# The first expert block is taken out of the block loop of a 32-expert layer and worked ahead of the block table

## What is computed

```
logits = (h @ w_router) + b_router            # [512, 32]
topv, idx = lax.top_k(logits, 4)
gates = softmax(topv)
# tokens grouped by expert; for every block of tokens of one expert e:
gu = xblk @ w_gate_up[e] + b_gate_up[e]       # 1024 -> 2048
gate, up = min(gu[:, :1024], 7), clip(gu[:, 1024:], -7, 7)
act = (up + 1) * gate * sigmoid(1.702 * gate)
y = act @ w_down[e] + b_down[e]               # 1024 -> 1024
out[token] += y * gate_weight
```

## Time and profile before

| | |
|---|---|
| median of 3 runs | 2981.27 us (2976.05 to 2981.37) |
| the profiled execution's own time | 2982.14 us |
| its span in the profile | 2980.3 us |
| TensorE busy | 2805.3 us, 94% |
| VectorE, ScalarE, GpSimd busy | 1319.7, 829.6, 103.1 us |
| read from and written to HBM | 572.91 MB, 29.88 MB |

### The profile page before, as it was taken

The page is one execution under the profiler, slowest core; times in us unless marked ns, Lnnn a source line. Parts: engine busy times, 40 slices in busy tenths (PEclk is TensorE's granted clock), DMA queues, the critical chain, the costliest instruction groups (busy, mean ns, idle before and its releaser), DMA issues.

```text
span 2980.3 us, 44597 instructions
## 1 busy us (share of the span) xinstructions
PE 2805.3 (94%) x16220; PEld 1781.0 (60%) x16221; DVE 1319.7 (44%) x2773; ACT 829.6 (28%) x1663; POOL 103.1 (3%) x118
## 2 busy tenths in 40 slices
PE   9999999988999989998999899999999999999999
PEld 7888668743333333333333387585787695666884
DVE  6774686442232222222222455535564454444662
ACT  3321662212222222222222223414121224323211
POOL 0000000000000000000000000011000000110000
PEclk9999999978999999999999999999999999999999
DMA  3224312257999999999999831031321321112212
GB/s 143 85 71 138 120 52 85 76 209 317 416 423 415 414 410 410 414 413 407 412 413 413 337 117 69 29 110 36 106 85 57 105 101 43 68 64 78 85 57 85
DMA packets 115239, 587.90 MB, mean 197 GB/s; under 512 B 12714, under 2 KB 18218, under 8 KB 89507
## 3 DMA queue, kind: packets, MB, share of 16 engines
q1 hardware_dynamic: 105890, 569.26, 48.4%
q0 software_dynamic: 9216, 16.90, 1.5%
HBM read 572.91 MB, written 29.88 MB: 202 GB/s over the span
## 4 chain that ended last, share of the span: by engine, by line
PE 80%; DMA 12%; DVE 5%; issue 2%; ACT 2%; DVEq 1%; ACTq 0%; SPq 0%; POOLq 0%
PE banks L422 37%; DMA arena<-in_w_experts 11%; PE banks L1757 11%; PE banks L355 5%; PE banks L1799 5%; PE banks L989 4%; PE banks L916 3%; PE banks L1765 2%; PE banks L1805 2%; PE banks L1004 2%; PE banks L978 2%; PE banks L294 1%; PE banks L1243 1%; PE banks L952 1%; PE banks L1736 1%
## 5 line engine op out<-in xcount | busy, mean ns | idle before, releaser
L422 PE MATMUL banks<-arena 128*128 128x256 f32 (+2 forms) x5376 | 1156.1, 376 | 12.7 <-ACT arena L459 6.0
L422 PEld LDWEIGHTS banks<-arena 128*128 128x128 f32 x5376 | 1005.4, 190 | 147.8 <-issue 14.1
L1757 PE MATMUL banks<-arena 128*64 128x512 f32 x2048 | 466.7, 601 | 48.4 <-DMA arena<-in_w_experts 34.2
L1757 PEld LDWEIGHTS banks<-arena 128*64 128x64 f32 x2048 | 156.2, 137 | 315.2 <-issue 313.0
L459 ACT ACTIVATE arena<-banks 128x512 f32<-128x512 f32 (+2 forms) x220 | 129.9, 590 | 699.5 <-PE banks L422 696.6
L407 DVE TENSOR_TENSOR arena<-arena 128x1024 f32<-128x1024 f32 (+2 forms) x220 | 235.8, 1072 | 50.6 <-issue 26.4
L1938 DVE TENSOR_TENSOR arena<-banks,arena 128x512 f32<-128x512 f32 x64 | 44.3, 692 | 462.7 <-PE banks L1783 236.5
L1799 PE MATMUL banks<-arena 128*64 128x512 f32 x1024 | 237.8, 600 | 1.6 <-DMA arena<-in_w_experts 1.1
L475 DVE TENSOR_TENSOR arena<-banks,arena 128x512 f32<-128x512 f32 (+2 forms) x123 | 83.5, 680 | 273.6 <-PE banks L422 269.8
L355 PE MATMUL banks<-arena 128*128 128x512 f32 x384 | 166.8, 592 | 0.0
L1799 PEld LDWEIGHTS banks<-arena 128*64 128x64 f32 x1024 | 67.6, 135 | 129.1 <-issue 129.1
(11 more groups left out here) (269 smaller groups left out, 2388.3 us busy)
## 6 DMA issues: line engine op xcount, KB each, us to landing
arena<-in_w_experts SPq DMA_DIRECT2D x192, 2048.0 KB, 24.1
arena<-in_w_in SPq DMA_DIRECT2D x76, 1024.0 KB, 4.9
arena<-in_w_out SPq DMA_DIRECT2D x12, 1024.0 KB, 5.0
arena<-in_w_branch SPq DMA_DIRECT2D x24, 512.0 KB, 4.6
expert_rows<-arena SPq DMA_DIRECT2D x1, 8192.0 KB, 30.2
arena<-expert_rows SPq DMA_DIRECT2D x4, 2048.0 KB, 18.0
arena<-in_w_in SPq DMA_DIRECT2D x2, 2048.0 KB, 9.1
arena<-in_w_in SPq DMA_DIRECT2D x4, 832.0 KB, 4.9
```

The lines of the kernel that those rows point to most:

```text
L422: last = PE.matmul(PS[:, bank, t * width:(t + 1) * width], one[:, t * P:(t + 1) * P], other, start=(first and t == 0 and kk == 0), stop=(t ...
L1757: last = PE.matmul(PS[HB * s:HB * (s + 1), 4 + h], xT[:, k, 0:HB], gate_up(2 * h + s, k), start=(k == 0), stop=(k == 7))
```

## The change

Block 0 is expert 0's, column 0 of the lists, whatever the router gives; so only whether it has few rows and the number of blocks are needed for it. A new semaphore `first_rdy` says that these two are there, and TensorE, ScalarE and GpSimd start the expert stage on it. VectorE waits for `listed` earlier, turns column 0 first and the other 191 columns after `first_rdy`. TensorE's part of the table (`rank_kinds`, `spread_keys`, `turn_gates`, `rows_of_table`) is spread over the start of block 0: behind the first turns, and in the middle and at the end of block 0's first group of products. `block(0)` is written out ahead of the loop, which now runs over 1 to `final`. The sums for `Gm` move behind `keys_rdy`. The gates of the last block's expert no longer come from a product with a one-hot matrix (`ONE_E`): ScalarE's copy is stored to memory (`GATES_T`, 64 KB), SyncE reads the expert's row back to 96 partitions of `SEL` ahead of its loop, and VectorE makes `SEL` and `DIAG` in the last block (`last_gates`). SyncE still waits for `table_rdy` ahead of its loop. A cut diff:

```diff
+        GATES_T = nc.dram_tensor("gates_of_experts", [NE, S], F32, kind="Internal").ap()
...
+        def rank_kinds(pe):
+
+            pe.wait_ge(SEM["kinds_rdy"], up(1))
+            PE.matmul(PS[:, 1, 200:202], v(CO["before"], P), v(KINDS, 2), start=True, stop=True)
+            PE.matmul(PS[:, 1, 202:204], v(CO["ones"], P), v(KINDS, 2), start=True, stop=True).then_inc(SEM["ranked"], 1)
+
+        def spread_keys(pe):
+
+            pe.wait_ge(SEM["keys_rdy"], up(1))
+            PE.matmul(PS[:, 1, 256:384], v(CO["ones"], P), v(KEYS, P), start=True, stop=True).then_inc(SEM["keys_mm"], 1)
+
+        def rows_of_table(pe):
+
+            pe.wait_ge(SEM["column_rdy"], up(1))
+            for q, col in enumerate((FOUND, FOUND + 4, FOUND + 5)):
+                last = PE.matmul(PS[0:1, 1, 64 * q:64 * q + 64], v(col, 1), v(PLACES, 64), start=True, stop=True)
+            last.then_inc(SEM["row_mm"], 1)
+
+        def turn_gates(pe):
+
+            pe.wait_ge(SEM["gmat_rdy"], up(1))
+            for tt in range(TT):
+                gates = v(R + 1536 + NE * tt, NE)
+                PE.transpose(PS[0:NE, 6, tt * P:(tt + 1) * P], gates, ident)
+                last = PE.matmul(PS[BS:P, 7, tt * P:(tt + 1) * P], gates, ident, start=True, stop=True, tile_position=(0, BS))
+            last.then_inc(SEM["gt_mm"], 1)
...
-                pe.wait_ge(SEM["gmat_rdy"], up(1))
-                for tt in range(TT):
-                    PE.transpose(PS[0:NE, 2, tt * P:(tt + 1) * P], Gm[:, tt], ident)
-                    last = PE.matmul(PS[BS:P, 3, tt * P:(tt + 1) * P], Gm[:, tt], ident, start=True, stop=True, tile_position=(0, BS))
-                last.then_inc(SEM["gt_mm"], 1)
-                pe.wait_ge(SEM["kinds_rdy"], up(1))
-                PE.matmul(PS[:, 1, 200:202], v(CO["before"], P), v(KINDS, 2), start=True, stop=True)
-                PE.matmul(PS[:, 1, 202:204], v(CO["ones"], P), v(KINDS, 2), start=True, stop=True).then_inc(SEM["ranked"], 1)
-                pe.wait_ge(SEM["keys_rdy"], up(1))
-                PE.matmul(PS[:, 1, 256:384], v(CO["ones"], P), v(KEYS, P), start=True, stop=True).then_inc(SEM["keys_mm"], 1)
-                pe.wait_ge(SEM["column_rdy"], up(1))
-                for q, col in enumerate((FOUND, FOUND + 4, FOUND + 5)):
-                    last = PE.matmul(PS[0:1, 1, 64 * q:64 * q + 64], v(col, 1), v(PLACES, 64), start=True, stop=True)
-                last.then_inc(SEM["row_mm"], 1)
...
-                act.wait_ge(SEM["gt_mm"], up(1))
-                AC.activation(v(GT, S, NE), PS[0:NE, 2], ACT.Copy)
-                AC.activation(v(SEL, S, NE, BS), PS[BS:P, 3], ACT.Copy).then_inc(SEM["gt_rdy"], 1)
...
+                V.memset(v(BE, 1, 1), 0.0)
+                V.memset(v(BCOL, 1, 1), 0.0)
...
-                V.tensor_tensor(tmp, oh, v(GATES, 16).unsqueeze(2).to_broadcast([P, 16, NE]), ALU.mult)
-                V.drain()
-                V.tensor_reduce(Gm, v3(R + 896, TT, 4, NE).rearrange("p t k e -> p t e k"), AX.X, ALU.add)
-                V.drain().then_inc(SEM["gmat_rdy"], 1)
...
+                def rows_of_lists(first, n):
+                    nobody, found_, rows_, tokens = (v(o + first, n) for o in (R + 1856, TAB + 1024, ALLR, ALLT))
+                    V.tensor_scalar(nobody, PS[:, 0, first:first + n], 0.0, float(1 << 20), ALU.is_equal, ALU.mult)
+                    V.drain()
+                    V.scalar_tensor_tensor(found_, PS[:, 0, first:first + n], -1.0, nobody, ALU.add, ALU.add)
+                    V.drain()
+                    V.tensor_copy(rows_.bitcast(I32), found_)
+                    V.drain()
+                    V.tensor_scalar(tokens.bitcast(I32), rows_.bitcast(I32), 2, None, ALU.logical_shift_right)
+                    V.drain()
+                dve.wait_ge(SEM["listed"], up(1))
+                rows_of_lists(0, 1)
+                V.tensor_copy(v(TOK, 1).bitcast(I32), v(ALLT, 1).bitcast(I32)).then_inc(SEM["tok_rdy"], 1)
                 V.tensor_copy(cnt, PS[:, 1, 128:160])
...
-                nobody = v(R + 256, LISTS)
-                dve.wait_ge(SEM["listed"], up(1))
-                V.tensor_scalar(nobody, PS[:, 0, 0:LISTS], 0.0, float(1 << 20), ALU.is_equal, ALU.mult)
-                V.drain()
-                V.scalar_tensor_tensor(v(R + 512, LISTS), PS[:, 0, 0:LISTS], -1.0, nobody, ALU.add, ALU.add)
-                V.drain()
-                V.tensor_copy(v(ALLR, LISTS).bitcast(I32), v(R + 512, LISTS))
-                V.drain()
-                V.tensor_scalar(v(ALLT, LISTS).bitcast(I32), v(ALLR, LISTS).bitcast(I32), 2, None, ALU.logical_shift_right)
-                V.drain()
-                V.tensor_copy(v(TOK, 1).bitcast(I32), v(ALLT, 1).bitcast(I32)).then_inc(SEM["tok_rdy"], 1)
+                V.tensor_scalar(v(FEW, 1, 1).bitcast(I32), cnt[0:1, 0:1], float(P // 2), None, ALU.is_le)
+                V.tensor_scalar(v(LAST, 1, 1).bitcast(I32), cum[0:1, NE - 1:NE], -1.0, None, ALU.add)
+                V.drain().then_inc(SEM["first_rdy"], 1)
+                rows_of_lists(1, LISTS - 1)
...
+                V.tensor_tensor(tmp, oh, v(GATES, 16).unsqueeze(2).to_broadcast([P, 16, NE]), ALU.mult)
+                V.drain()
+                V.tensor_reduce(Gm, v3(R + 896, TT, 4, NE).rearrange("p t k e -> p t e k"), AX.X, ALU.add)
+                V.drain().then_inc(SEM["gmat_rdy"], 1)
                 dve.wait_ge(SEM["keys_mm"], up(1))
...
-                V.tensor_copy(v(BE, 192, 1).bitcast(I32), PS[0:1, 1, 0:192])
-                V.tensor_scalar(v(LAST, 1, 1).bitcast(I32), cum[0:1, NE - 1:NE], -1.0, None, ALU.add)
+                V.tensor_copy(v2(BE, 3, 64, 1).bitcast(I32)[:, :, 1:64], PS[0:1, 1, 0:192].rearrange("p (a b) -> p a b", a=3)[:, :, 1:64])
                 V.drain().then_inc(SEM["table_rdy"], 1)
...
+                sp.wait_ge(SEM["gt_rdy"], up(1))
+                sp.dma_start(GATES_T, v(GT, S, NE)).then_inc(SEM["gates_out"], 16)
                 sp.wait_ge(SEM["table_rdy"], up(1))
                 norm_pre.lead(sp, c)
                 final = last_block(sp)
+                e_last = entry(sp, BE, final, NE - 1)
+                sp.wait_ge(SEM["gates_out"], 16)
+                sp.dma_start(v(SEL, S, BS), GATES_T[bass.ds(e_last, 1)].rearrange("o t -> (o t)").partition_broadcast(BS)).then_inc(SEM["share_in"], 16)
                 with sp.Fori(1, final + 1) as j:
...
-                pe.wait_ge(SEM["table_rdy"], up(1))
+                pe.wait_ge(SEM["first_rdy"], up(1))
                 final = last_block(pe)
...
                 gather_T(1)
-                pe.wait_ge(SEM["one_rdy"], up(1))
-                pe.wait_ge(SEM["gt_rdy"], up(1))
-                PE.matmul(PS[:, 7], v(ONE_E, P, NE), v(GT, S, NE), start=True, stop=True).then_inc(SEM["share_mm"], 1)
-                with pe.Fori(0, final + 1) as j:
+                rank_kinds(pe)
+
+                def block(j):
+                    first = isinstance(j, int)
                     few = entry(pe, FEW, j, 1)
...
-                        pe.wait_ge(SEM["sel_made"], up(1))
...
-                                last = products(h, ks)
+                                if first and h + kh == 0:
+                                    products(h, ks[:2])
+                                    spread_keys(pe)
+                                    turn_gates(pe)
+                                    last = products(h, ks[2:])
+                                    rows_of_table(pe)
+                                else:
+                                    last = products(h, ks)
                                 if more:
                                     last = more_products(h, ks)
                                 last.then_inc(SEM["ch_free"], 2)
+                                if first and h and not kh:
+                                    pe.wait_ge(SEM["table_rdy"], up(1))
                         turn_products(1, more)
                         gather_T(j + 2)
+                        if first:
+                            pe.wait_ge(SEM["gt_rdy"], up(1))
                         down(more)
 
                     with pe.If(few > 0):
                         rows_of_block(False)
                     with pe.Else():
                         rows_of_block(True)
+                block(0)
+                with pe.Fori(1, final + 1) as j:
+                    block(j)
 
                 pe.wait_ge(SEM["bdown_in"], 16)
+                pe.wait_ge(SEM["sel_made"], up(1))
...
-                act.wait_ge(SEM["table_rdy"], up(1))
+                act.wait_ge(SEM["first_rdy"], up(1))
                 final = last_block(act)
...
                 copy_T(1)
+                act.wait_ge(SEM["gt_mm"], up(1))
+                AC.activation(v(GT, S, NE), PS[0:NE, 6], ACT.Copy)
+                AC.activation(v(SEL, S, NE, BS), PS[BS:P, 7], ACT.Copy).then_inc(SEM["gt_rdy"], 1)
                 with act.Fori(0, final + 1) as j:
...
+                    act.wait_ge(SEM["table_rdy"], up(1))
...
```

(39 more changed lines are left out.)

## The result

The changed kernel took 2988.32 us in the median (6 runs, 2987.32 to 2993.26), the kernel before beside it 2980.49: a ratio of 1.0034, 95% interval 1.0022 to 1.0047. It is slower by 8 us by the medians and 10 by the ratio, and outside the range that was forecast. The profiled execution took 2989.23 us round a span of 2987.4.

What follows compares the result with a forecast made beforehand. The expert stage was taken to be bound by its DMA weight stream, so by that stream's start. Terms -0.9 - 0.7 + 0.6 = -1.0 us gave 2981.1, or 2980.3 against the median, which was taken; range 2974 to 2986.5 us.

Steps and rivals of the forecast that it cites:

- Steps 1 to 5: From the list products to SyncE's first issue in its loop: issue at 689.7 us instead of 690.6, 0.9 won.
- Step 6: Start of the weight stream: chunk 1 is already free, so the gap at 692 to 694 us closes, winning 0.7.
- Step 7: Gates through memory, 64 KB out and 96 x 2 KB in: costs the full stream 0.6 us, latency hidden.
- step 8: VectorE's work for the last block, moved into that block: costs nothing; without cover at most 9.6 us.
- Step 9: Gather of block 1: lands at 694 us or later; costs nothing, or a few us on TensorE.
- Rival D: Block 0's jump into the loop: a code stall moves the first issue 4.4 us, to 694.1; 2984.7 us; chance 0.10.
- D2: The same code pause at every turn of the expert loop: about +95 us, 3075 us; chance 0.03.
- the step behind the sum: Block 0's first group: TensorE frees it at 684.6 instead of 690.6 us, 6 sooner, which the stream cannot use.
- Rival C: TensorE sets the expert stage's end: products starting 8.4 us sooner reach the end, 2972.9 us; chance 0.08.
- One of the signs given for being right: Expert stage: TensorE's waits for weights start one block pair sooner, their sum larger by about 5 us.

Runs made afterwards that it cites:

- gates_only: The kernel before, with only the last block's gates sent through memory and made by VectorE in the last block; 2982.28 us, ratio 1.0006 to before.
- late_tok: The changed kernel with VectorE's wait for the next gather and its token copy moved behind each block's first activation half; 2984.25 us, ratio 1.0014 to before.
- one_branch: The changed kernel with block 0's second TensorE branch (many rows) and its test left out; 2981.56 us, ratio 1.0009 to before.
- few_last: The changed kernel with late_tok's edit and block 0's two TensorE branches swapped, few rows' code last; 2984.23 us, ratio 1.0014 to before.
- loop0: The changed kernel with block 0 back in the loop and the table's small products together ahead of it; 2983.31 us, ratio 1.0015 to before.
- sp_late: The kernel before, with SyncE entering its loop only when block 0 has freed three chunks instead of one; 2985.74 us, ratio 1.0018 to before.

## Why the prediction was wrong

Steps 1 to 5, the road to the first issue: right, and about 1 us optimistic. `tok_rdy` 665.4 (665.6 forecast), `first_rdy` 667.3 (667.7), products 676.9 (675.6; the gather released TensorE at 673.7, within the bound of 673.9 that was given, not at the 672.5 that was taken), gates turned at 684.1 (682.1), table at 686.8 (685.9), first issue 690.80 (689.7).

Step 6, the hole closed: in part, the share from 692 to 694 us is 0.85 instead of the 0.65 of the earlier trace rows. Step 7, the added transfers, and step 8, the last block's work: nothing to be seen, by gates_only.

Step 9 is the one that failed. It said of the next gather "nothing, or a few us on TensorE, which is 6 us ahead and does not set the end". I had the gather landing late (from 694; it landed at 699) and asked only when TensorE wants its rows. But VectorE waits for it first, ahead of block 0's activation. VectorE's timeline after, from 684 to 704 us:

```profile
688.53 0.15 DVE L1943 COPY arena<-arena 128x1 int32 x1 [1.77 <-issue]
...
698.99 0.15 DVE L1972 COPY arena<-arena 128x1 int32 x1 [9.25 <-DMA arena<-h_rows,arena]
699.46 0.69 DVE L1981 TENSOR_TENSOR arena<-banks,arena 128x512 f32<-128x512 f32 x1 [0.32 <-issue]
```

The tokens of block 1 are set behind the table, and the gather is issued at 689.54 and releases VectorE 9.5 us later, in company with the stream. Until then the activation is held up, by it ScalarE's sigmoid, by that ScalarE's next copy, and by that TensorE's turn. This cost 5.0 us more than before, at a place where the lateness does reach the end, and late_tok takes it away.

Rival D had the right mechanism with the wrong place and price. I priced the code pause only where it would delay the first issue, and gave it 0.10; it came twice behind that point, 6.3 us at the entry of block 1 instead of 4.4, and 4.7 us ahead of block 2. The sum had no term for these 6.6 us, nor for the 3.3 us of lower clock behind the waits. That the measured 2988.32 lies near D's 2984.7 is no merit of D: its first issue at 694.1 did not happen. D2, a pause at every turn, did not happen. The Trainium skill ("Runtime: NRT & Kernel Launch", Instruction fetch mechanics) says that a taken branch to code outside what has been fetched must first fetch it; the runs agree as far as they go: the pauses moved with the order of the branches, and the DMA's instruction queue moved 9 blocks of 16 KB from 700 to 800 us after the change, 3 before and 4 in one_branch. From 800 to 1600 us it moved none in either kernel, and there no pause of TensorE without a shown cause is over 0.7 us. That a given pause is one such fetch is argued, not shown: in the time of some pauses a block was moved (3.61 us after the change, 3.83 us in few_last), in that of others none (4.38 us before, 4.71 us after). Nor is new code needed: before, the pause of 4.38 us stands ahead of block 1, which runs the same branch as block 0 had (the timeline has no products of L1765 in either). Why loop0 pauses ahead of block 2 and the kernel before does not, with the same loop, stays open.

What made both misses count was the step behind the sum: that TensorE frees its first group 6 us sooner "does not count, because the stream cannot use it". Read the other way round this says that TensorE may also be late at no cost, and that is false. The stream was the bound of the kernel before, as forecast and as sp_late shows, but TensorE's bound stood only about 2 us below it. The sign was in the profile: the chain lies on TensorE up to 972 us while the DMA share is 0.99. In numbers: the first issue moved by +0.2, block 3 by +11.1, of which 2 were cover, so that the two bounds give +9, and found was +10.2. Rival C, that TensorE sets the end, had 0.08; after the change TensorE does set it, by being late and not, as C had it, by being early. One of the signs given for being right came out reversed and says the same: TensorE's waits for weights were to grow by about 5 us and fell from 34.2 to 28.7.

## What to carry to other kernels

When two resources are both near full in a stage, work out the bound of each, and how far the second lies below the first: it is the second that says what a delay may cost. Follow a moved hand-over past its first user, to everything that stands behind the wait in that engine's queue, and look at who starts competing with it for the same transfers. A block written out ahead of a loop moves the code as well as the work: here the pauses at the first turns moved with the order of the branches, and one of them fell where the engines had least slack. An engine that has stood still for some us may also come back at a lower clock, as here (0.50 and 0.63), which makes each wait dearer than its length.

## What was unexpected of the hardware

TensorE's pauses at the first turns and jumps were 2.7 to 5.9 us each, also at a moment (677 to 680 us, few_last) when the weight stream had not yet begun, so they do not need its traffic. The pause at the loop's first turn is not fixed for the same loop: 4.4 us before, 5.1 in sp_late, 5.9 in gates_only. The same gather of block 1 took 4.1 us from issue to landing before, when nothing else was in flight, and released VectorE 9.5 us after its issue when the stream's first chunks were issued 1.3 us behind it.
